# Delta rule in a two-block kernel: diagonal blocks of two directions moved by one transfer, sent back ahead of head 3's rows, and beta scalings split between ScalarE and VectorE

## The reference, cut to what matters

```python
g = jnp.cumsum(g, axis=-1)
decay = where(tri, exp(g[..., :, None] - g[..., None, :]), 0)
kb = k * beta[..., None]
a_mat = where(strict, einsum('bhncd,bhnsd->bhncs', kb, k) * decay, 0) + eye(C)
rhs = concatenate([v * beta[..., None], kb * exp(g)[..., None]], axis=-1)
sol = triangular_solve(a_mat, rhs, lower=True, unit_diagonal=True)
u, w = sol[..., :Dv], sol[..., Dv:]
intra = einsum('bhncd,bhnsd->bhncs', q, k) * decay
def step(S, inp):
    v_new = u_c - w_c @ S
    o = (q_c * exp(g_c)) @ S + a_c @ v_new
    S = S * exp(g_last) + (k_c * exp(g_last - g_c)).T @ v_new
```

## Time and profile before

| what | value |
|---|---|
| median of 3 runs | 2832.3 us (2832.14 to 2832.37) |
| the profiled execution | 2832.62 us, its span 2830.8 us |
| TensorE, VectorE, ACT, GpSimd busy | 2679.3, 1174.1, 1072.3, 1243.0 us of the span |
| in-projection | 0 to 440 us |
| first attention | 440 to 595.5 us |
| delta rule | 595.5 to about 818 us |
| second inverse on GpSimd | 639.3 to 676.5 us |
| granted TensorE clock, mean | 0.977 of full speed |

### The profile page before, as it was taken

The page is one execution under the profiler, slowest core; times in us unless marked ns, Lnnn a source line. Parts: engine busy times, 40 slices in busy tenths (PEclk is TensorE's granted clock), DMA queues, the critical chain, the costliest instruction groups (busy, mean ns, idle before and its releaser), DMA issues.

```text
span 2830.8 us, 33041 instructions
## 1 busy us (share of the span) xinstructions
PE 2679.3 (95%) x13337; PEld 2150.5 (76%) x13337; DVE 1174.1 (41%) x1631; ACT 1072.3 (38%) x1593; POOL 1243.0 (44%) x717
## 2 busy tenths in 40 slices
PE   6999998988969999999999999899999999999997
PEld 4778875667858888887888777666788888788885
DVE  6465666655663222222222327667532222222223
ACT  4443445634544422233322333656443222232222
POOL 2222222554026555556555554311455454565554
PEclk8999998989989999999999999999999999999998
DMA  3222415441143222223222232100222222323331
GB/s 132 90 88 96 150 45 203 135 142 52 38 145 115 97 97 97 97 97 104 97 97 97 98 130 91 40 8 1 99 95 98 97 97 97 112 90 108 116 103 69
DMA packets 93880, 273.20 MB, mean 97 GB/s; under 512 B 25944, under 2 KB 26136, under 8 KB 93600
## 3 DMA queue, kind: packets, MB, share of 16 engines
q1 hardware_dynamic: 93728, 271.09, 28.2%
HBM read 240.05 MB, written 31.00 MB: 96 GB/s over the span
## 4 chain that ended last, share of the span: by engine, by line
PE 82%; DVE 6%; POOL 5%; ACT 3%; DMA 2%; issue 1%; SPq 1%; POOLq 0%; DVEq 0%; ACTq 0%
PE ps L350 23%; PE ps L351 23%; PE ps L352 23%; PE ps L875 2%; ACT t L366 2%; PE ps L895 2%; PE ps L859 2%; POOL t L1336 1%; POOL t L1333 1%; PE ps L491 1%; DVE t L1009 1%; PE ps L1437 1%; POOL t L1834 1%; POOL t L415 1%; ACT t L958 1%
## 5 line engine op out<-in xcount | busy, mean ns | idle before, releaser
L366 ACT ACTIVATE t<-t 128x1024 fp32r<-128x1024 f32 (+5 forms) x961 | 735.3, 810 | 1392.1 <-PE ps L352 650.6
L415 POOL TENSOR_TENSOR t<-t 128x1024 fp32r<-128x1024 f32 x356 | 862.5, 2427 | 874.7 <-ACT t L366 874.6
L350 PE MATMUL ps<-t 128*128 128x512 f32 (+1 forms) x3034 | 1199.0, 395 | 47.5 <-DVE t L528 18.4
L352 PE MATMUL ps<-t 128*128 128x512 f32 (+1 forms) x3034 | 1181.4, 389 | 0.0
L351 PE MATMUL ps<-t 128*128 128x512 f32 (+1 forms) x3034 | 1181.3, 389 | 0.0
L350 PEld LDWEIGHTS ps<-t 128*128 128x128 f32 x3034 | 572.0, 189 | 184.8 <-issue 53.0
L351 PEld LDWEIGHTS ps<-t 128*128 128x128 f32 x3034 | 572.5, 189 | 120.7 <-issue 6.5
L352 PEld LDWEIGHTS ps<-t 128*128 128x128 f32 x3034 | 571.9, 188 | 118.5
L2050 DVE SCALAR_TENSOR_TENSOR t<-ps,t 128x512 f32<-128x512 f32 x192 | 132.7, 691 | 315.0 <-PE ps L352 277.2
L2106 POOL TENSOR_TENSOR t<-t 128x512 fp32r<-128x512 f32 x84 | 108.7, 1295 | 332.4 <-ACT t L366 332.4
L2027 DVE TENSOR_TENSOR t<-ps,t 128x512 f32<-128x512 f32 x84 | 58.1, 692 | 396.2 <-PE ps L352 396.2
(11 more groups left out here) (167 smaller groups left out, 1884.6 us busy)
## 6 DMA issues: line engine op xcount, KB each, us to landing
t<-in_wts_dram SPq DMA_DIRECT2D x356, 512.0 KB, 3.5
t<-pj SPq DMA_DIRECT2D x39, 512.0 KB, 5.9
pj<-t SPq DMA_DIRECT2D x32, 512.0 KB, 2.7
t<-in_rpb_dram SPq DMA_DIRECT2D x8, 736.0 KB, 7.7
t<-in_xT_dram SPq DMA_DIRECT2D x8, 512.0 KB, 10.5
t<-grow_d SPq DMA_DIRECT2D x8, 512.0 KB, 8.4
t<-beta_d SPq DMA_DIRECT2D x8, 512.0 KB, 9.5
t<-in_xT_dram SPq DMA_DIRECT2D x16, 256.0 KB, 4.0
```

The lines of the kernel that those rows point to most:

```text
L350: e.matmul(out, ah, bh, start=start, stop=False)
L352: return e.matmul(out, al, bh, start=False, stop=stop)
L366: return e.activation(out, in_, fn, scale=scale)
L415: e.tensor_tensor(lo[:], T.raw[n % NR][:], hi[:].bitcast(F), SUB).then_inc(*w_lo.up(n))
```

## The change

- `D_.R` and `D_.Y` of a head's two directions (for heads 0 and 1: of all four chains) lie in one array, in a new order of the buffers, so that one transfer can take the blocks of two or four chains. The gather has 8 transfers instead of 16 for each batch, the scatter 4 for batch 0 and 8 for batch 1 instead of 16. The first of a head's gathers now waits for both of its directions.
- In the attention, SP issues `sp_blocks_out` of batch 0 and head 3's rows ahead of park 2 and of the load of q of head 3.
- GpSimd starts batch 0's inverse at step 19 instead of 20, with two columns instead of three in each fourth step, and multiplies by the gate of pair 2 at step 35 instead of 30. Head 2's rows come at step 34 instead of 37.
- Head 2's differences (VectorE) come at step 32 instead of 33, its exponentials (ACT) in step 34 of the attention loop instead of at the start of the delta stage.
- Of the scalings by beta, those of the backward direction (d = 1) are done by VectorE, in one product of 128x1024 with beta repeated along the row; those of the forward direction stay on ACT.
- In the delta stage SP issues the load of kt of head 0 behind the second gather and the load of its blocks.

```diff
--- before.py
+++ after.py
@@ -261,7 +261,8 @@
     D_ = Tiles()
     early = ExitStack()
     D_.dm = sb(early, [128, 4, 128], side="right")
-    D_.R, D_.Y, D_.D = ([[sb(early, [128, L], side="right") for _ in range(2)] for _ in range(2)] for _ in range(3))
+    D_.D = [[sb(early, [128, L], side="right") for _ in range(2)] for _ in range(2)]
+    D_.RR, D_.YY = [sb(early, [128, 4, L], side="right")], [sb(early, [128, 4, L], side="right")]
     D_.k = [sb(early, [128, L], side="right") for _ in range(2)]
 
     N_ = Tiles()
@@ -276,18 +277,20 @@
 
     with ExitStack() as st:
         two_heads = lambda: [[sb(st, [128, L]) for _ in range(2)] for _ in range(2)]
-        one_head = lambda: [[sb(st, [128, L]) for _ in range(2)]]
         D_.k += [sb(st, [128, L]) for _ in range(2)]
-        D_.R, D_.Y = D_.R + one_head(), D_.Y + one_head()
+        D_.RR.append(sb(st, [128, 2, L]))
+        D_.YY.append(sb(st, [128, 2, L]))
         D_.var = [sb(st, [128, 24]) for _ in range(4)]
         sb(st, [128, 800])
         D_.vt = [sb(st, [128, L]) for _ in range(4)]
         D_.D += two_heads()
-        D_.R = D_.R + one_head()
+        D_.RR.append(sb(st, [128, 2, L]))
         sb(st, [128, 896])
-        D_.Y = D_.Y + one_head()
+        D_.YY.append(sb(st, [128, 2, L]))
         D_.X = two_heads() + two_heads()
         D_.blocks = [sb(st, [128, L]) for _ in range(3)]
+        D_.R, D_.Y = ([[T[0][:, 2 * h + i, :] for i in range(2)] for h in range(2)] + [[t[:, i, :] for i in range(2)]
+                                                                                   for t in T[1:]] for T in (D_.RR, D_.YY))
     early.close()
     gates.close()
 
@@ -1091,17 +1094,20 @@
                 na_large(e, w, c, x)
         act_attention(e, w, NA, prep, lambda i: act_delta_early(e, w, i))
 
+
+    NA_GATES = [14, 22, 35, 38]
+
     def pool_na(e, w):
         for i in range(len(na_pairs) + 8):
             pool_attention(e, w, NA, i)
             for c, x in na_prep.get(i, []):
                 na_small(e, w, c, x)
             pool_delta_early(e, w, i)
-            if i == 37:
+            if i == 34:
                 for d in range(2):
                     scaled_row(e, w, 2, d)
-            if i >= 14 and (i - 14) % 8 == 0:
-                c = (i - 14) // 8
+            if i in NA_GATES:
+                c = NA_GATES.index(i)
                 w.wait_ge(NA.out, 2 * c + 1)
                 w.wait_ge(na_load[c % 2][3], c)
                 e.tensor_tensor(X[:, c, :], X[:, c, :], N_.raws[c % 2][3], MUL).then_inc(*na_gate.up(c))
@@ -1163,12 +1169,12 @@
             e.dma_start(D_.k[h][:], pj[20 + h]).then_inc(*h_load["k"][h].up(h))
         w.wait_ge(NA.value, (11, 1))
         e.dma_start(q_first[2], pj[18]).then_inc(*q_load[0].up(2))
-        park(2)
-        e.dma_start(q_first[3], pj[19]).then_inc(*q_load[1].up(3))
         sp_blocks_out(e, w, 0)
         w.wait_ge(NA.top, (last_pair(3), 1))
         w.wait_ge(NA.turn, na_pairs[-1].last + (0,))
         sp_rows(e, w, 3)
+        park(2)
+        e.dma_start(q_first[3], pj[19]).then_inc(*q_load[1].up(3))
         park(3)
 
 
@@ -1184,7 +1190,7 @@
     (d_kk, d_qk, d_tr, d_xt, l_p, l_x, l_y, s_p1, s_p2, s_p3, s_po, o_turn) = kinds("delta_pe", 12)
     (d_exp, d_r1, d_x0, d_kd, d_tb, s_vn, s_oa, o_sq, o_ln, o_rs, o_rs2) = kinds("delta_act", 11)
     (d_diff, d_mt, d_in, l_p1, l_x1, l_y1, s_r, s_S, s_O, o_add, o_var, o_f0, o_f1, o_n,
-     o_out) = kinds("delta_dve", 15)
+     o_out, d_tb_v) = kinds("delta_dve", 16)
     d_zero, d_db, i_ini_p, i_mul_p, i_sub_p = kinds("delta_pool", 5)
     slots_d = ring([slot(i) for i in range(4)])
     slots_l = ring([slot(i) for i in range(2)])
@@ -1211,7 +1217,7 @@
     early_diff = lambda i: divmod(i - 3, 2) if 3 <= i < 11 else None
     early_exp = lambda i: divmod((i - 5) // 2, 2) if 5 <= i < 13 and (i - 5) % 2 == 0 else None
     early_row = lambda i: divmod((i - 6) // 2, 2) if 6 <= i < 14 and (i - 6) % 2 == 0 else None
-    first_inverse, inverse_rate = 20, 3
+    first_inverse, inverse_rate = 19, [2, 3, 3, 3]
     P1 = [X[:, 4, :], X[:, 5, :]]
     kt_at = [3, 6, 7, 3]
     q_at = [2, 6, 7, 3]
@@ -1252,7 +1258,14 @@
                     m = e.matmul(o, D_.k[h][:, c], right[:, c], start=True, stop=True)
             m.then_inc(*{"kk": d_kk, "qk": d_qk, "tr": d_tr}[what].up((h, u)))
 
+    def decays(e, w, h):
+        for d in range(2):
+            w.wait_ge(d_diff, (h, d))
+            act(e, D_.D[h][d][:], D_.D[h][d][:], ACT.Exp).then_inc(*d_exp.up((h, d)))
+
     def act_delta_early(e, w, i):
+        if i == 34:
+            decays(e, w, 2)
         if early_exp(i):
             h, d = early_exp(i)
             w.wait_ge(d_diff, (h, d))
@@ -1265,7 +1278,7 @@
                 d_r1.note(h)
 
     def dve_delta_early(e, w, i):
-        if i == 33:
+        if i == 32:
             differences(e, w, 2)
         if early_diff(i):
             n, part = early_diff(i)
@@ -1312,7 +1325,7 @@
         if i == first_inverse:
             pool_inverse[0] = blocks(e, w, 0)
         if first_inverse <= i < first_inverse + 16:
-            for _ in range(inverse_rate):
+            for _ in range(inverse_rate[i % 4]):
                 next(pool_inverse[0], None)
 
     pool_inverse = [None]
@@ -1356,17 +1369,23 @@
             e.dma_start(D_.k[h][:], pj[20 + h]).then_inc(*h_load["k"][h].up(h))
         sp_rows(e, w, 1)
 
-    def block_of(b, a, i):
-
-        return lambda dram: dram[b].rearrange("(g t b) (j i) -> g b j t i", t=8, b=4, i=32)[a, i]
+    def blocks_of(dram, b, first, count, i):
+
+        return dram[b].rearrange("(g t b) (j i) -> g b j t i", t=8, b=4, i=32)[first:first + count, i].rearrange(
+            "g j t i -> j g t i")
+
+    def diagonal(T, i):
+        k = slice(32 * i, 32 * i + 32)
+        return T.rearrange("p g (t f) -> p g t f", t=8)[k, :, :, k]
 
     def sp_gather(e, w, b):
-        for a in range(4):
-            h, d = chain(b, a)
-            w.wait_ge(*((d_mt, (h, d)) if d == 0 else (d_r1, h)))
+        for x in range(2):
+            h = 2 * b + x
+            w.wait_ge(d_mt, (h, 0))
+            w.wait_ge(d_r1, h)
+            T = D_.RR[0][:, 2 * h:2 * h + 2, :] if b == 0 else D_.RR[h - 1][:]
             for i in range(4):
-                k = slice(32 * i, 32 * i + 32)
-                e.dma_start(block_of(b, a, i)(rb_d), v8(D_.R[h][d])[k, :, k]).then_inc(*gath.up((b, a, i)))
+                e.dma_start(blocks_of(rb_d, b, 2 * x, 2, i), diagonal(T, i)).then_inc(*gath.up((b, x, i)))
         gath.note(b)
 
     def sp_blocks_in(e, w, b):
@@ -1381,12 +1400,12 @@
         w.wait_ge(*last_block[b])
         e.dma_start(wb_d[b], inverted[b]).then_inc(*wb_store.up(b))
         w.wait_ge(wb_store, b)
-        for a in range(4):
-            h, d = chain(b, a)
-            w.wait_ge(d_zero, (h, d))
+        for h in (2 * b, 2 * b + 1):
+            w.wait_ge(d_zero, (h, 1))
+        for x, T in enumerate([D_.YY[0][:]] if b == 0 else [D_.YY[1][:], D_.YY[2][:]]):
+            n = 4 if b == 0 else 2
             for i in range(4):
-                k = slice(32 * i, 32 * i + 32)
-                e.dma_start(v8(D_.Y[h][d])[k, :, k], block_of(b, a, i)(wb_d)).then_inc(*scat.up((b, a, i)))
+                e.dma_start(diagonal(T, i), blocks_of(wb_d, b, n * x, n, i)).then_inc(*scat.up((b, x, i)))
         scat.note(b)
 
     def pe_delta(e, w):
@@ -1465,7 +1484,7 @@
                 for a, h, d in cs:
                     key, c = (h, d, n), at(d)
                     p = place(r, ("2",) + key, [(s_vn, key)])
-                    w.wait_ge(d_tb, (h, d))
+                    w.wait_ge(d_tb_v if d else d_tb, (h, d))
                     if n:
                         w.wait_ge(s_r, key)
                     else:
@@ -1558,6 +1577,9 @@
             if what == "XY" or d == 0:
                 w.wait_ge(l_y, key)
                 e.tensor_tensor(Y_[:], Y_[:], r[("y",) + key], SUB).then_inc(*l_y1.up(key))
+            if what == "F" and d == 1:
+                w.wait_ge(l_x1, key)
+                e.tensor_tensor(v8(X_), v8(X_), bcl(beta[:, :, hd_of(h, d)]), MUL).then_inc(*d_tb_v.up((h, d)))
 
         def scan(b, r, between):
             for n in range(8):
@@ -1636,11 +1658,6 @@
                 finish(h, part)
 
     def act_delta(e, w):
-        def decays(h):
-            for d in range(2):
-                w.wait_ge(d_diff, (h, d))
-                act(e, D_.D[h][d][:], D_.D[h][d][:], ACT.Exp).then_inc(*d_exp.up((h, d)))
-
         def backward(h):
             w.wait_ge(d_tr, h)
             act(e, D_.R[h][1][:], slots_d["tr", h], ACT.Copy).then_inc(*d_r1.up(h))
@@ -1661,8 +1678,8 @@
                 for t in range(8):
                     m = act(e, D_.R[h][d][:, tok[t]], X[:, kt_at[h], tok[t]], ACT.Copy, scale=ed[:, t, hd:hd + 1])
                 m.then_inc(*d_kd.up((h, d)))
-            if what == "F":
-                w.wait_ge(*((l_y1, (h, d, 1)) if d == 0 else (l_x1, (h, d, 1))))
+            if what == "F" and d == 0:
```

(6 more changed lines are left out.)

## The result

The changed kernel takes 2818.8 us (median of 4 runs, 2816.9 to 2820.0) against 2832.3 us before (4 runs, 2832.1 to 2836.0): a ratio of 0.9947, 95% interval 0.9933 to 0.9961, or -11 to -19 us. A second measurement beside other runs of the kernel before gave 2820.7 (5 runs) and 0.9958 (0.9945 to 0.9970). It is faster, as forecast, but by some 13.5 us (the difference of the medians) and not by 8.9.

The account below looks back on a forecast made before the run. TensorE's idle time in 440 to 818 us, some 59 us, was taken as all that can be won. Terms -5.9 + 0.2 - 3.6 + 2.2 - 1.8 = -8.9 gave a 2823.5 us median, range 2818.5 to 2828.5.

Parts of the forecast that it names:

- The first inverse: GpSimd's batch 0 inverse during the attention, started at step 19: 0.4 us off TensorE's 1.94 us stall, inverse ending at 583.8.
- Where that stall goes: TensorE's wait for the first scatter: VectorE's head 2 product releases the last first transpose instead; -7.2, charged to -5.9 us.
- The charge of 1.3 for the clock: TensorE after about 3 us idle at the first transposes: a lower granted clock loses 1.3 us of the gain.
- The second gather and scatter: SP's transfers for heads 2 and 3: doubled gather transfers cost +0.2, 8 scatter issues instead of 16 give -3.6 us.
- Beta on VectorE: Delta stage: two VectorE products delay GpSimd's second inverse by +2.2 us; for heads 2 and 3 -1.8.
- The end, -1.8: Before the second scan, heads 2 and 3: less scaling on ACT shortens TensorE's wait, -1.8 us (-1.0 to -3.5).
- Grouping does save: Against the rival that grouping saves nothing, as packets take the time or the clock stays low: -5.3, 2827.0 us; chance 0.22.
- the slower rival: Gather and scatter: grouped transfers run on few DMA engines, +24.2, 2856.5 us; chance 0.04.
- nothing disturbs: Rival: GpSimd runs on beside VectorE's two products and the clock holds over the 3 us idle: -12.4, 2819.9 us; chance 0.18.
- One sign of being wrong: SP's grouped transfers: the prediction is wrong if grouped issues take over 0.5 us each.

Follow-up runs that it names:

- second pair: A second profile each of the unaltered kernel before and the changed kernel; these repeats took 2832.9 us and 2820.7 us.
- first pair: The first profiles of the kernel before and the changed kernel, whose measured medians were 2832.3 us and 2818.8 us.
- late send: Changed kernel with pair 2's gate product right behind the first inverse, and park 2 and head 3's q ahead of the block store again: 2822.4 us, 0.9963.

## Why the prediction was right in sign and too small

- **The first inverse** is the step that failed. "At step 24 the counts are 14 columns against 12 ... I take 0.4" looked at one diagonal and its 1.94 us. The next one, 12 columns later, paces the attention's end, and the new rates take a column out in front of it: 1.7 us more. The row of before didn't show this wait because the low clock covered it; a second profile of the same kernel does. Terms: -0.4 forecast, -2.2 measured in the second pair. The 0.4 itself was right: from GpSimd's diagonal product of step 20 to that of step 24 it took 23.6 us in the four profiles that start at 20 and 23.0 to 23.1 in the ten that start at 19. The other 1.1 us ahead of the diagonal in the first pair were there at step 20's product already (535.93 against 534.88) and are missing in the second pair.
- **Where that stall goes** was right in mechanism and, but for the clock, in size. VectorE's last product releases the transposes, they end 8.98 us behind the attention's end where the text has 8.8 to 9.3, and the gain is 6.8 to 6.9 us. The charge of 1.3 for the clock has the right size (1.4), but it isn't paid each time and wasn't in either profile of the changed kernel. Head 2's rows didn't move against the attention's end, as forecast: the first product waits for ACT ([4.47 <-ACT] at 592.84, 0.9 us behind TensorE's 591.96, and 0.9 in the kernel before), so the place of the gate product is nothing to them, as the late send showed.
- **The second gather and scatter**: -3.3 for -3.6. The gather costs 0.5 for 0.2 (6.6 us against 6.1 from head 3's transposes to the load, both at 1.97 us for eight). The store took 2.6 instead of 3.1 and 3.5, which the sum didn't have; over the other kernels it took 2.6 to 3.1 in no order that I can explain.
- **Beta on VectorE**: +1.7 for +2.2. By the Trainium skill (SBUF — State Buffer, Who interferes with whom), by which the second of the two instructions is blocked until the first is done, the prediction had estimated 2.4. The runs agree in kind, but the measured delay is 0.86 us for each product, and GpSimd's begins only when VectorE's has run for 0.5 us or so. The end, -1.8, measured -2.3 to -2.6; with all of beta on ACT the piece takes 136.1 us, so 1.4 to 1.8 of it are the beta edit's and the remaining 0.6 to 0.9 weren't separated.
- **The rivals.** Grouping does save (3.3), so the slower rival is out: the grouped kernels' eight transfers have landed 5.8 us after the first issue. The Trainium skill (DMA: Bandwidth & Descriptors, Why a DMA increments its semaphore by 16 and not by 1), by which 32 partitions outermost keep all 16 engines in use, agrees with that. The rival "nothing disturbs" was wrong on GpSimd and, as it came out, right on the clock.
- **The missing 4.5 us**, by the second pair, are 1.7 behind the diagonal, 1.4 up to head 3 (the clock's charge, which wasn't paid), 0.8 ahead of the second scatter (the shorter store and the smaller price of beta, less what gather and scatter cost more) and 0.5 at the end. Only the first is a wait that the prediction didn't have; the others are terms of the wrong size.
- **One sign of being wrong** stood at its edge: grouped issues were to take at most 0.5 us each, and the eight took 4.04, 0.04 more for each than single ones.

Corrected, the sum is -2.2 - 6.8 + 0.5 - 0.5 (the store) - 3.3 + 1.7 - 2.4 = -13.0, against -13.5 to -13.8 in the profiles. What stays open is about 1 us between one execution and the next, ahead of the diagonal, and the gain of the early send in the changed kernel, which the profile puts at nothing and the times between nothing and 4 us.

## What to carry to other kernels

When background work is spread between deadlines of a stage, count it in front of each deadline and not only the first that shows a wait, since a wait can be covered in one profile by a slower clock on the waiting engine. Two edits that relieve the same wait (an earlier send and fewer issues) don't add up; their worth is that of the next thing that is late. Work handed to an idle engine is free only where nothing on the critical path is slowed by it (here two VectorE products cost GpSimd's inverse 1.7 us), so it can be worth doing for one batch and not for the other.

## What the runs showed of the hardware

- The granted clock behind an idle time is not the same twice. Behind 1.83 to 1.94 us at the diagonal it was 0.77, 0.89, 0.89 and 1.00 over 560 to 575 us; behind 1.36 to 1.53 us it was 1.00 in all ten profiles. Behind 3.2 us the next eight transposes took 1.10, 1.50 or 1.97 us.
- On SP's queue a transfer of four times the blocks was issued in 0.57 to 0.62 us where one took 0.45 (4 issues in 2.24 us, 8 in 4.04, 16 in 7.72), so fewer and larger transfers paid.
- VectorE's 16 differences took 4.28 us alone and 7.05 beside GpSimd's two gate products of 128x1024, and these were no longer for it (4.72 us for two, 4.66 to 4.70 in other kernels). At other places it was GpSimd that paid: a row product took 3.16 instead of 2.36 beside VectorE, a product of the inverse 1.51 instead of 0.65.
